# Three transformer layers on one core: attention results that come out turned, with the probabilities scaled ahead of the product

## The chip, the cores and the metric

The kernel runs on one core of a Trainium2 chip. The metric is the device time of one execution in microseconds (us). One execution computes a whole forward pass of three layers for one sequence of 256 rows and width 1024.

The core has five engines with a queue each: TensorE (PE in the rows; its weight loads are PEld), VectorE (DVE), ScalarE (ACT), GpSimd (POOL) and SyncE (SP), which issues the loads of the weights. They meet only through semaphores. TensorE writes to PSUM, eight banks of 128 partitions x 512 f32.

## The reference, cut to what matters

There are four attentions. All have 256 queries and 256 keys.

```
moba   8 heads of 64,  causal        \  first layer
cross  4 heads of 256, no mask       /
dsa    8 heads of 64,  causal and a learned choice of keys   second layer
mla   16 heads of 64 (scores over 96), causal                third layer

p = softmax(scores)               # over the keys
o = p @ v                         # per head
x = x + rms_norm(concat(o) @ w_out)
```

The first layer has a retention beside moba (4 heads of 128), whose result goes through a norm of each head and a gate, and the second one a short convolution with a gate beside dsa. Each shares the output projection with its attention: half of the rows of `w_out` belong to each. An MLP follows in each layer.

## The kernel before, in words

**Rows and tokens.** The 256 tokens are two tiles (`t` = 0, 1) of 128. An activation has its tokens on the partitions, `x[:, t, :]`. A projection needs it turned, with the features on the partitions: `hT[:, chunk, token]`, eight chunks of 128 features. TensorE turns blocks of 128 x 128 against an identity (`turn`, L1658), four of them to one PSUM bank; ScalarE and VectorE take them out.

**Large products.** A number is split in two fp32r numbers, hi and lo, and each product is made three times: hi x hi, lo x hi, hi x lo (`products`, L1589). Turned activations come as `hT_hi` (ScalarE, L603) and `hT_lo` (VectorE, L1077: PSUM less hi). Weights come by DMA in units of 128 x 2048 f32; ScalarE writes `w_hi` (L585), VectorE `w_lo` (L1056, L1059, L1062). `split_to(u)` in the lists of ScalarE and VectorE says where in their order this is done for unit u. Ring buffers hold four units.

**Attention** (`attention`, one function on each of PE, DVE and ACT). Each engine runs over the heads; these are the steps for a head `hd` of a causal attention, all in plain f32, of which TensorE makes two passes for each product (x2 in the counts of the rows):

1. PE `scores` (L1696): keys 0 to 127 for token tile 0, keys 0 to 255 for tile 1, so 384 columns in one PSUM bank (two banks in turn).
2. DVE (L1207): two instructions, of 128 and 256 columns, scale and mask the scores into SBUF (`S`), and take the row's extreme.
3. ACT (L748): two exponentials into `E`, with the sums of the rows in `a.sums`.
4. PE `turn_probs` (L1704), two heads behind the scores: three turns of 128 x 128 into a bank.
5. DVE `copy_turned` (L1219): 384 columns to `ET` in SBUF.
6. PE `values` (L1713), three heads behind: for each of the three blocks a product with 128 columns of `ET` as the stationary operand and the 64 columns of v as the moving one, into columns of the head in a bank with tokens on the partitions.

Cross has full blocks: four turns of a head, and four products with 256 moving columns. It takes the scores from PSUM, the extreme by L1211.

**Behind the last head.** The results in PSUM are unscaled. VectorE inverts the sums (L1236, L1253), and multiplies PSUM by them into `h` or `mix` in SBUF (L1237, L1255); TensorE turns these blocks (L1658), 8 for moba and dsa, 16 for cross and mla; ScalarE and VectorE write `hT_hi` and `hT_lo`; then the output projection runs (`project`, `out_project`). For cross and mla this is done in two halves of 512 features: the second one is turned behind the first unit of the projection. In moba the turns stand behind the first two score products of the retention (`meanwhile` in `retention`), in dsa within the projection, which begins with the convolution's features.

**Retention.** PE L1744 (scores) and L1752 (values), DVE L1369 (decay) between them. Then ACT squares (L869), DVE sums the squares of each head (L1375), POOL makes the inverse roots (L484, L485, 8 columns), DVE scales and gates (L1383), and PE turns the result within the output projection. The VectorE's list has a unit's `w_lo` (`split_to(n["used"] + 3)`, L1056) between L1375 and L1383.

**Convolution.** POOL makes three taps (`convolve`, L502 to L505). ACT copies the turned gate from PSUM (L947, into `gbT`), POOL multiplies (L507), ACT writes hi (L953), and POOL lo (L510).

**Latent rows of the third layer** (L1499 to L1540). DVE `copy_latents(t)` copies 384 query columns, and then waits for a norm by POOL (L522 to L525) before it writes the rest; `low_queries(1)` stands behind it in VectorE's list, and PE waits for that. POOL spreads a rotated key of 32 rows to 15 heads in one copy (L515).

What sets the order is written by hand: each engine's list, and the waits in it. `tb_ready` and `tb_free` hand the four turn banks (PSUM 4 to 7) round.

## Time and profile before

| | us |
|---|---|
| median of 3 runs | 1061.05 (1058.54 to 1062.13) |
| profiled execution | 1060.72 |
| its span, first to last instruction | 1058.9 |
| PE busy | 1032.3 (97%) |
| DVE busy | 647.0 (61%) |
| ACT busy | 565.5 (53%) |
| POOL busy | 85.4 (8%) |

The profiled execution took 1060.72 us; 1058.9 of these lie between its first and its last instruction. An engine's busy time is the sum of its instructions. For PE the ends of the instructions are modelled and overlap, so the distance between the starts of two groups says more than their durations. TensorE's granted clock was 0.996 of 2.4 GHz over the span.

### The profile page before, as it was taken

What the parts mean: (1) busy time and instruction counts of PE and PEld (TensorE: products, weight loads), DVE (VectorE), ACT (ScalarE), POOL (GpSimd) and SP (SyncE); (2) the same over time, 40 slices, a digit from 0 to 9 for tenths busy, and PEclk for the clock granted to TensorE, in tenths of its full rate; (3) what the DMA queues carried; (4) which work ended last, traced back from release to release, by engine and by line L of the source; (5) the groups of instructions that cost most, each with busy time, mean ns of one, the idle gap of its engine ahead of it and who ended that gap; (6) DMA issues with size and microseconds to landing.
All of it is one profiled execution on the core that took longest, in us unless ns stands there. A gap on an engine that the chain in (4) does not pass through costs nothing.

```text
span 1058.9 us, 13808 instructions
## 1 busy us (share of the span) xinstructions
PE 1032.3 (97%) x5074; PEld 867.6 (82%) x5074; DVE 647.0 (61%) x1007; ACT 565.5 (53%) x860; POOL 85.4 (8%) x109
## 2 busy tenths in 40 slices
PE   7999999999999999999999999999998999999997
PEld 6888878887888888788888888888897888888886
DVE  5575665446656455758846755455579767555553
ACT  7566455427545544756655744545466557454541
POOL 2010101001000000200061100000051000000000
PEclk9999999999999999999999999999999999999999
DMA  8746126414455454453433555544255035554521
GB/s 337 292 162 238 58 91 230 157 40 165 173 198 184 179 216 178 156 230 115 157 127 119 221 197 189 195 176 165 83 189 209 1 148 210 196 197 171 188 80 40
DMA packets 28461, 176.29 MB, mean 166 GB/s; under 512 B 3248, under 2 KB 3392, under 8 KB 9984
## 3 DMA queue, kind: packets, MB, share of 16 engines
q1 hardware_dynamic: 26784, 170.08, 43.6%
q0 software_dynamic: 1456, 5.48, 1.4%
q8 instruction: 29, 0.48, 0.2%
q10 hardware_dynamic: 176, 0.13, 0.0%
q14 instruction: 16, 0.13, 0.0%
HBM read 174.62 MB, written 1.05 MB: 166 GB/s over the span
## 4 chain that ended last, share of the span: by engine, by line
PE 90%; DVE 4%; ACT 2%; issue 2%; POOL 1%; DMA 1%; SPq 0%; DVEq 0%; ACTq 0%; POOLq 0%
PE PS L1589 77%; PE PS L1658 3%; PE PS L1696 3%; PE PS L1713 3%; PE PS L1803 2%; ACT w_hi L585 1%; PE PS L1704 1%; PE PS L1953 1%; DVE w_lo L1062 1%; DMA x<-in_x 1%; ACT work L665 0%; DVE w_lo L1059 0%; DVE w_lo L1056 0%; POOL rstd L485 0%; DVE arena L1095 0%
## 5 line engine op out<-in xcount | busy, mean ns | idle before, releaser
L1062 DVE SCALAR_TENSOR_TENSOR w_lo<-w_raw,gcol,w_hi 128x512 fp32r<-128x512 f32 (+4 forms) x318 | 261.2, 879 | 182.7 <-ACT w_hi L585 182.1
L585 ACT ACTIVATE w_hi<-w_raw,gcol 128x512 fp32r<-128x512 f32 (+4 forms) x326 | 244.5, 817 | 103.4 <-PE PS L1589 102.4
L1589 PE MATMUL PS<-w_hi,hT_hi 128*128 128x512 f32 (+2 forms) x888 | 243.4, 394 | 4.9 <-issue 2.4
L1589 PE MATMUL PS<-w_hi,hT_lo 128*128 128x512 f32 (+2 forms) x888 | 236.2, 386 | 0.0
L1589 PE MATMUL PS<-w_lo,hT_hi 128*128 128x512 f32 (+2 forms) x888 | 234.2, 384 | 0.2 <-DVE w_lo L1056 0.2
L1589 PEld LDWEIGHTS PS<-w_hi,hT_lo 128*128 128x128 f32 x888 | 165.6, 189 | 32.8
L1589 PEld LDWEIGHTS PS<-w_lo,hT_hi 128*128 128x128 f32 x888 | 164.9, 188 | 33.1 <-DVE w_lo L1056 0.6
L1589 PEld LDWEIGHTS PS<-w_hi,hT_hi 128*128 128x128 f32 x888 | 161.6, 190 | 35.8 <-DVE hT_lo L1077 1.9
L1056 DVE TENSOR_TENSOR w_lo<-w_raw,w_hi 128x2048 fp32r<-128x2048 f32 (+1 forms) x70 | 135.9, 1956 | 86.7 <-ACT w_hi L585 86.7
L585 ACT ACTIVATE w_hi<-w_raw 128x2048 fp32r<-128x2048 f32 (+1 forms) x70 | 114.6, 1644 | 109.4 <-PE PS L1589 109.4
L1589 PE MATMUL PS<-w_hi,gT_hi 128*128 128x512 f32 x408 | 113.9, 392 | 0.0
L1589 PE MATMUL PS<-w_lo,gT_hi 128*128 128x512 f32 x408 | 112.9, 390 | 0.0
L1589 PE MATMUL PS<-w_hi,gT_lo 128*128 128x512 f32 x408 | 112.7, 389 | 0.0
L1589 PEld LDWEIGHTS PS<-w_hi,gT_lo 128*128 128x128 f32 x408 | 76.6, 188 | 16.0
L1589 PEld LDWEIGHTS PS<-w_lo,gT_hi 128*128 128x128 f32 x408 | 76.5, 188 | 15.9
L1589 PEld LDWEIGHTS PS<-w_hi,gT_hi 128*128 128x128 f32 x408 | 76.2, 188 | 15.4
L484 POOL TENSOR_SCALAR msq<-ssq 128x1 f32<-128x1 f32 (+1 forms) x31 | 12.9, 418 | 823.2 <-ACT work L665 760.9
L603 ACT ACTIVATE hT_hi<-PS 128x512 fp32r<-128x512 f32 (+2 forms) x46 | 25.4, 582 | 42.7 <-PE PS L1658 42.7
L1077 DVE TENSOR_TENSOR hT_lo<-PS,hT_hi 128x512 fp32r<-128x512 f32 (+2 forms) x46 | 29.5, 668 | 26.8 <-ACT hT_hi L603 26.6
L748 ACT ACTIVATE work<-work,attention_bias 128x128 f32<-128x128 f32 x64 | 28.5, 447 | 26.0 <-DVE attention_bias L1207 26.0
L1141 DVE TENSOR_TENSOR work<-PS,gain 128x512 f32<-128x512 f32 x28 | 18.0, 684 | 39.7 <-ACT work L665 39.7
L665 ACT ACTIVATE work<-PS 128x1024 f32<-128x1024 f32 x14 | 14.4, 1028 | 49.7 <-PE PS L1589 49.7
(171 smaller groups left out, 811.5 us busy)
## 6 DMA issues: line engine op xcount, KB each, us to landing
w_raw<-in_w SPq DMA_DIRECT2D x64, 1024.0 KB, 4.8
w_raw<-in_w_gu SPq DMA_DIRECT2D x22, 1024.0 KB, 4.8
w_raw<-in_w_in SPq DMA_DIRECT2D x11, 1024.0 KB, 7.8
w_raw<-in_w_dn SPq DMA_DIRECT2D x22, 512.0 KB, 5.2
w_raw<-in_w_mem_k SPq DMA_DIRECT2D x4, 1024.0 KB, 4.8
w_raw<-in_w_out SPq DMA_DIRECT2D x4, 1024.0 KB, 4.8
w_raw<-in_w_cq SPq DMA_DIRECT2D x4, 1024.0 KB, 4.8
w_raw<-in_w_mem_v SPq DMA_DIRECT2D x4, 1024.0 KB, 4.8
```

The lines of the kernel that those rows point to most:

```text
L585: ins = act.activation(high, source, ACT.Copy, scale=1.0 if col is None else gcol[:, col + TURNED * k:col + TURNED * k + 1])
L603: act.activation(d, PS[:, 4 + n["tb"] % 4, 0:blocks * P].rearrange("p (b m) -> p b m", m=P), ACT.Copy).then_inc(tb_high, 1)
L748: ins = act.activation(a.E[hd % 3][:, c0:c1], src, ACT.Exp, bias=a.nb[:, hd, t:t + 1], scale=-1.0 if a.masked else a.scale, accum_out=a.su ...
L1056: ins = dve.tensor_tensor(lo, raw, hi, ALU.subtract)
L1062: ins = dve.scalar_tensor_tensor(out=lo, in0=raw, scalar=gcol[:, col + TURNED * k:col + TURNED * k + 1], in1=hi, op0=ALU.mult, op1=ALU.sub ...
L1077: dve.tensor_tensor(lo, PS[:, 4 + n["tb"] % 4, 0:blocks * P].rearrange("p (b m) -> p b m", m=P), hi.bitcast(F32), ALU.subtract).then_inc(t ...
L1141: steps.mark(dve.tensor_tensor(work[:, 2 * t + i, :], PS[:, 2 * t + i, :], gain[:, g, cols], ALU.mult))
L1589: mm = pe.matmul(bank(t, j)[:, 0:width], rows[:, kc0 + k, tok], w[:, s, at:at + width], start=begin and i == 0, stop=end and i == 2)
L1658: mm = pe.transpose(PS[0:rows, 4 + n["tb"] % 4, i * P:(i + 1) * P], src, ident[:])
L1696: mm = pe.matmul(PS[:, a.score_bank + hd % 2, c0:c1], q, k, start=i == 0, stop=i == len(pairs) - 1)
L1713: mm = pe.matmul(out_banks(a, t)[:, hd * a.dv:(hd + 1) * a.dv], a.ET[hd % 2][:, c0 + s * P:c0 + (s + 1) * P], a.v(hd, s), start=s == 0, st ...
L1803: mm = pe.transpose(m.turn_bank[t][:, b * P:(b + 1) * P], hidden[:, t, b * P:(b + 1) * P], ident[:])
```

## The change

The products of probabilities and values swap their operands. Two names need an explanation: `a.lag` is the number of heads by which `turn_probs` stands behind the scores (3 for causal attentions, 2 for cross), `a.ring` the number of buffers.

- VectorE inverts the sums of each head (`invert`), and GpSimd multiplies the head's probabilities in place by them (`normalise`, two instructions of a head), before TensorE turns them.
- The products have v as the stationary operand. For heads of 64, two heads share a group: one goes to partitions 0 to 63 of the result, the other to 64 to 127. The moving columns are 256 and 128 of `ET`. For cross the stationary operand is 128 columns of v and the moving one 256 columns of `ET`.
- The result lies in PSUM with features on the partitions. ScalarE writes `hT_hi` from it (`high_results`), VectorE `hT_lo` (`low_results`). The multiplications by the sums, the rows in `h` and `mix`, and their 48 turns are gone.
- `S` is gone: DVE writes masked scores to `E`, and ACT the exponentials in place. `E` and `ET` have four buffers each in causal attentions (three `S`, three `E` and two `ET` before), three each in cross.
- Retention: `split_to(n["used"] + 3)` stands before the sums of squares in VectorE's list. The turns of the memory's key rows are in two parts, around the turns of the retention's result.
- Convolution: DVE multiplies by the gate straight from PSUM, between two heads; ACT writes hi in two instructions and DVE lo in two, in place of POOL's five.
- Latent rows: the copy of the query columns and `low_queries(1)` stand before the wait for the norm. The rotated key is spread in five copies of three heads. `attention(mla, [0])` stands before `split_to(e + 9)` in VectorE's list.

```diff
@@ Attention @@
-                scored = 3 * width if causal_blocks else 0
-                self.S, self.E, self.ET = slots(0, 3), slots(scored, 3), slots(scored + 3 * width, 2)
+                self.ring = 4 if causal_blocks else 3
+                self.lag = 3 if causal_blocks else 2
+                self.group = P // dv if dv < P else 1
+                self.banks = heads * dv // 256
+        def result_bank(a, b):
+            return PS[:, a.out_bank + b, :].rearrange("p (c m) -> p c m", m=SEQ)
+        def result_rows(tile, b):
+            return tile[:, 2 * b:2 * b + 2, :]
@@ gpsimd @@
-                pool.wait_ge(gate_copied, TT)
-                pool.tensor_tensor(y_conv, y_conv, gbT, ALU.mult).then_inc(conv_ready, 1)
-                for c in range(4):
-                    pool.wait_ge(conv_high, c + 1)
-                    pool.tensor_tensor(hT_lo[:, 4 + c, :], y_conv[:, c, :], hT_hi[:, 4 + c, :].bitcast(F32), ALU.subtract).then_inc(conv_low, 1)
+            def normalise(a):
+                for hd in range(a.H):
+                    pool.wait_ge(a.inverted, hd + 1)
+                    for t in range(TT):
+                        place = a.E[hd % a.ring][:, slice(*a.cols[t])]
+                        ins = pool.tensor_scalar(place, place, a.sums[:, hd, t:t + 1], None, ALU.mult)
+                    ins.then_inc(a.normed, 1)
-                pool.tensor_copy(kT4[64:96, 1:16, :], kT4[64:96, 0:1, :].to_broadcast([32, 15, SEQ])).then_inc(rope_spread, 1)
+                for head in range(1, 16, 3):
+                    pool.tensor_copy(kT4[64:96, head:head + 3, :], kT4[64:96, 0:1, :].to_broadcast([32, 3, SEQ])).then_inc(rope_spread, 1)
@@ scalar @@
+            def high_results(a, banks=None):
+                for b in banks or range(a.banks):
+                    act.wait_ge(a.summed, (b + 1) * a.H // a.group // a.banks)
+                    act.activation(result_rows(hT_hi, b), result_bank(a, b), ACT.Copy).then_inc(a.high, 1)
...
-            attention(mla, range(2, mla.H), False)
-            high_halves(hT_hi)
+            attention(mla, range(2, 8), False)
+            for b in range(2):
+                attention(mla, range(8 + 4 * b, 12 + 4 * b), False)
+                high_results(mla, [b])
+            high_results(mla, [2, 3])
@@ vector @@
+                def invert(hd):
+                    dve.wait_ge(a.probs, hd + 1)
+                    dve.reciprocal(a.sums[:, hd, :], a.sums[:, hd, :]).then_inc(a.inverted, 1)
...
-                for hd in heads or range(a.H + 2):
+                for hd in heads or range(a.H + a.lag):
                     if hd < a.H:
                         masked_max(hd)
-                    elif rows is not None:
-                        normalise_half(a, rows, hd - a.H, 0)
-                    if hd >= 2:
-                        copy_turned(hd - 2)
+                    if 1 <= hd <= a.H:
+                        invert(hd - 1)
+                    if hd >= a.lag:
+                        copy_turned(hd - a.lag)
+            def low_results(a, banks=None):
+                for b in banks or range(a.banks):
+                    dve.wait_ge(a.high, b + 1)
+                    dve.tensor_tensor(result_rows(hT_lo, b), result_bank(a, b), result_rows(hT_hi, b).bitcast(F32),
+                                      ALU.subtract).then_inc(a.low, 1)
@@ retention @@
                 if hd == 1:
-                    low_banks(2, half_rows(0))
+                    low_results(moba)
+            split_to(n["used"] + 3)
             for t in range(TT):
                 dve.wait_ge(ret_sq, t + 1)
                 dve.tensor_reduce(...)
-            split_to(n["used"] + 3)
@@ dsa @@
-            attention(dsa, range(dsa.H + 2), False)
-            normalise(dsa, h)
+            attention(dsa, range(5), False)
+            for t in range(TT):
+                dve.wait_ge(gate_turned, t + 1)
+                dve.wait_ge(convolved, 1)
+                dve.tensor_tensor(y_conv[:, :, token_cols(t)], PS[:, t, :].rearrange("p (b m) -> p b m", m=P), y_conv[:, :, token_cols(t)],
+                                  ALU.mult).then_inc(conv_ready, 1)
+            attention(dsa, range(5, dsa.H + dsa.lag), False)
+            for t in range(TT):
+                dve.wait_ge(conv_high, t + 1)
+                dve.tensor_tensor(hT_lo[:, 4:8, token_cols(t)], ..., ALU.subtract).then_inc(conv_low, 1)
+            low_results(dsa)
@@ latent rows @@
+            copy_queries(0)
             copy_latents(0)
...
+            copy_queries(1)
+            low_queries(1)
             copy_latents(1)
-            low_queries(1)
@@ tensor @@
                 def turn_probs(hd):
-                    pe.wait_ge(a.probs, hd + 1)
+                    pe.wait_ge(a.normed, hd + 1)
...
+                def values(g):
+                    pe.wait_ge(a.copied, a.group * (g + 1))
+                    if a.masked:
+                        for s in range(2):
+                            for i in range(2):
+                                hd = 2 * g + i
+                                mm = pe.matmul(result_bank(a, g // 2)[64 * i:64 * i + 64, g % 2, P * s:SEQ], a.v(hd, s),
+                                               a.ET[hd % a.ring][:, 2 * P * s:SEQ + P * s], start=s == 0, stop=s == 1)
+                    else:
+                        probs = a.ET[g % a.ring].rearrange("p (t s m) -> p t s m", t=TT, s=2)
+                        for i in range(2):
+                            for s in range(2):
+                                mm = pe.matmul(result_bank(a, g)[:, i, :], a.v(g, s)[:, P * i:P * i + P], probs[:, :, s, :],
+                                               start=s == 0, stop=s == 1)
                     mm.then_inc(a.summed, 1)
-                for hd in heads or range(a.H + 3):
+                for hd in heads or range(a.H + a.lag + 1):
                     if hd < a.H:
                         scores(hd)
-                    if 2 <= hd < a.H + 2:
-                        turn_probs(hd - 2)
-                    if hd >= 3:
-                        values(hd - 3)
-                    if rows is not None and hd == a.H + 1:
-                        turn_half(rows, 0)
+                    if a.lag <= hd < a.H + a.lag:
+                        turn_probs(hd - a.lag)
+                    done = hd - a.lag
+                    if done >= 1 and done % a.group == 0:
+                        values(done // a.group - 1)
...
+            def results(a, banks):
+                return lambda: pe.wait_ge(a.low, banks)
+            def out_project(a):
+                project(4, 2, wide, hooks={(0, 0): results(a, 2), (0, 2): results(a, 3), (0, 3): results(a, 4), (1, 2): tile0})
```

## Rows read from the trace of the kernel before

**Rows 1.** Page, busy time; and the chain that ended last, by engine.
```profile
PE 1032.3 (97%) x5074; PEld 867.6 (82%) x5074; DVE 647.0 (61%) x1007; ACT 565.5 (53%) x860; POOL 85.4 (8%) x109
PE 90%; DVE 4%; ACT 2%; issue 2%; POOL 1%; DMA 1%; SPq 0%; DVEq 0%; ACTq 0%; POOLq 0%
```
**Rows 2.** Busy us (x count) of PE, PEld, DVE, ACT, POOL in four stretches.
```profile
107.09:118.42 11.33, 11.30 (x89) 10.50 (x90) 6.86 (x28) 7.56 (x25) 0.00 (x0) 1.00 0.17 71
125.17:136.37 11.20, 8.68 (x52) 7.08 (x50) 8.12 (x15) 3.48 (x6) 3.82 (x2) 0.99 0.26 95
546.80:558.90 12.10, 12.06 (x97) 11.26 (x97) 6.68 (x27) 8.57 (x27) 5.21 (x5) 1.00 0.00 1
819.03:845.12 26.09, 25.55 (x202) 23.72 (x202) 17.87 (x73) 14.67 (x58) 0.00 (x0) 1.00 0.01 5
```
**Rows 3.** Timeline of one head in mla: start, duration, engine, line, idle before.
```profile
828.03 0.49 PE L1704 MATMUL PS<-ident,work 128*128 128x128 f32 x3
828.23 0.29 DVE L1207 CUSTOM_DVE_ANT_0 work<-PS,causal 128x128 f32<-128x128 f32 x1 [0.54 <-PE PS L1696]
828.25 0.75 PEld L1713 LDWEIGHTS PS<-arena,work 128*128 128x128 f32 x6
828.36 0.78 PE L1713 MATMUL PS<-arena,work 128*128 128x64 f32 x6
828.79 0.55 DVE L1219 COPY work<-PS 128x384 f32<-128x384 f32 x1
828.98 0.87 PE L1696 MATMUL PS<-arena 128*128 128x128 f32 x4
829.43 0.19 ACT L748 ACTIVATION_READ_ACCUMULATOR work<-work,attention_bias 128x1 f32 x1
829.69 0.49 PE L1704 MATMUL PS<-ident,work 128*128 128x128 f32 x3
```
**Rows 4.** Timeline of the end of cross, PE and DVE.
```profile
211.39 1.89 PE L1713 MATMUL PS<-arena,work 128*128 128x256 f32 x8
213.12 0.60 PE L1704 MATMUL PS<-ident,work 128*128 128x128 f32 x4
213.32 0.18 DVE L1236 RECIPROCAL attention_sum<-attention_sum 128x4 f32<-128x4 f32 x1 [2.85 <-PE PS L1713]
214.88 1.99 PE L1713 MATMUL PS<-arena,work 128*128 128x256 f32 x8 [1.16 <-DVE work L1219]
216.71 1.04 PE L1658 MATMUL PS<-ident,h 128*128 128x128 f32 x8
217.58 1.89 PE L1713 MATMUL PS<-arena,work 128*128 128x256 f32 x8
```
**Rows 5.** The chain that ended last, about retention and mla's projection: start, us, what.
```profile
127.45 2.18 POOL msq L484
129.70 1.66 POOL rstd L485
849.65 1.93 ACT w_hi L585
```
**Rows 6.** Timeline of mla's projection, TensorE's weight loads, idle before them.
```profile
846.55 0.30 PEld L1589 LDWEIGHTS PS<-w_hi,hT_hi 128*128 128x128 f32 x2 [0.24 <-DVE h L1237]
853.95 0.77 PEld L1589 LDWEIGHTS PS<-w_lo,hT_hi 128*128 128x128 f32 x4 [0.58 <-DVE w_lo L1056]
```
**Rows 7.** Groups of GpSimd by line.
```profile
L505 POOL TENSOR_TENSOR arena<-arena 128x1020 f32<-128x1020 f32 x1 | 4.3, 4301 | 0.1
L505 POOL TENSOR_TENSOR arena<-arena 128x1016 f32<-128x1016 f32 x1 | 2.0, 1992 | 0.1
L551 POOL MEMSET arena<- 128x2048 f32 x1 | 1.8, 1820 | 44.6 <-ACT arena L910 44.6
```
**Rows 8.** Timeline of the latent rows, before mla.
```profile
787.30 0.59 PE L1589 MATMUL PS<-w_hi,hT_hi 128*128 128x384 f32 x2 [0.97 <-DVE hT_lo L1077]
795.10 5.86 DVE L1059 SCALAR_TENSOR_TENSOR w_lo<-w_raw,gcol,w_hi 128x512 fp32r<-128x512 f32 x4
```

More of the change, by code:

```diff
@@ L542, in _ @@
             norms(TT)
+            normalise(moba)
             inverse_root(128, RETENTION, 8, ret_ss, TT, ret_rstd)
-            for _ in range(3):
+            for i in range(3):
                 norms(2 * TT)
                 load_gain()
+                if i == 0:
+                    normalise(cross)
             for i in range(2):
@@ L1360, in _ @@
             split_to(n["used"] + 2)
-            attention(moba, range(1, moba.H + 2), False)
+            attention(moba, range(1, moba.H + moba.lag), False)
             dve.wait_ge(decay_loaded, 16)
-            normalise(moba, mix)
             for hd in range(4):
@@ L1398, in _ @@
             split_to(n["used"] + 2)
-            attention(cross, range(1, cross.H + 2), False, h)
+            attention(cross, range(1, cross.H + cross.lag), False)
+            low_results(cross)
             split_to(n["used"] + 3)
-            out_rows(cross)
             boundary(1, 4)
@@ L1553, in _ @@
             copy_values(0)
+            attention(mla, [0])
             split_to(e + 9)
-            attention(mla, [0])
             copy_keys(1)
@@ L1558, in _ @@
             copy_values(1)
-            attention(mla, range(2, mla.H + 2), False, h)
-            out_rows(mla)
+            attention(mla, range(2, 13), False)
+            low_results(mla, [0])
+            attention(mla, range(13, 17), False)
+            low_results(mla, [1])
+            attention(mla, range(17, mla.H + mla.lag), False)
+            low_results(mla, [2, 3])
             boundary(5, 4)
@@ L1683, in turn_stream, with attention @@
                     turn([x[:, t, P * (4 * half + b):P * (4 * half + b + 1)] for b in range(4)])
-            def attention(a, heads=None, rows=None):
+            def attention(a, heads=None):
                 def scores(hd):
@@ L1931, in _ @@
             copied()
-            attention(cross, range(3, cross.H + 3), h)
-            out_project(h)
+            attention(cross, range(3, cross.H + cross.lag + 1))
+            out_project(cross)
             mlp(ffn, between={(2, 0): half_of(0, 0)})
@@ L2073, in _ @@
             pe.wait_ge(values_copied, 4)
-            attention(mla, range(3, mla.H + 3), h)
-            out_project(h)
+            attention(mla, range(3, mla.H + mla.lag + 1))
+            out_project(mla)
             mlp(mlps[1])
```

142 lines of the change are left out of this document (54 added, 88 removed).

## Prediction

> **What bounds the kernel now.** I read the page's busy times and chain first: TensorE is busy for 97% of the span and is 90% of the chain that ended last [rows 1]. So the change is worth what it takes from TensorE's queue, or from the waits in it, and VectorE, ScalarE and GpSimd have room to give. The table by stretch says the same of the four attentions: in moba, dsa and mla TensorE idles for 0.03, 0.04 and 0.54 us. The one large hole is the output projection behind the retention, 2.52 of 11.20 us [rows 2]. Then the timeline of one head in mla's steady part gives the prices [rows 3]: turns of the probabilities 828.03 to 828.36 (0.33 us), values 828.36 to 828.98 (0.62), scores 828.98 to 829.69 (0.71). That is 1.66 a head, 3.31 a pair, with no gap.
>
> Three prices of a pass follow. Eight turns of 128 columns take 216.71 to 217.58, 0.109 each. In cross eight passes of 256 columns take 211.39 to 213.12, 0.216 each [rows 4]. So a pass streams at 0.85 ns a column. But a value pass of only 64 columns costs 0.62 / 6 = 0.103, not 0.054 [rows 3]: its 128 stationary columns must be loaded, and that sets its pace. That is what the change turns round.
>
> **Values of a head of 64.** After it, a pair of heads needs for each head two passes of 256 columns and two of 128, with 64 stationary columns: 2 x (2 x 0.216 + 2 x 0.108) = 1.30 us if all stand one behind another. Before it was 1.24. So by itself the swap gains nothing; the point is the two halves of the columns. In program order the passes are A A B B (256 columns), A A B B (128). If a pass of one half may run beside one of the other, but each starts in order, this takes three slots of 0.216 and two of 0.108: 0.86 us. No row of before shows two passes side by side. The bounds are 0.65 (full overlap) and 1.30 (none); a price above 1.30 is a rival below. I take 0.86, since nothing in the order of the passes needs more.
>
> The Trainium skill (TensorEngine Tiling (Array Packing), Key Properties) says that tiles run in parallel, but also that a change of the tiling mode drains TensorE, which this change does twice a pair; the second rival stands beside that.
>
> **VectorE and the order in a pair.** VectorE needs 0.56 us for the extremes of a head and 0.55 for the copy (828.23 to 828.79, and the copy) [rows 3], and now a reciprocal: 0.18 with its latency for 4 columns [rows 4], I take 0.10 to 0.18 of its queue. That is 1.25 to 1.3 a head, 2.6 a pair, below TensorE's 2 x (0.71 + 0.33) + 0.86 = 2.94. But the values of a pair wait for the copy of its second head. From the end of the scores before: 0.2 to VectorE's start, 0.56 + 0.1 + 0.55 and 0.1 back, 1.5, against 0.33 + 0.71 + 0.33 = 1.37 of TensorE's work. So some 0.15 of stall: 3.09 a pair, a gain of 0.22.
>
> **GpSimd.** A head of 384 columns in two instructions. Memset writes 2048 columns in 1.82 us, 0.89 ns a column; a product with two inputs takes 1.99 for 1016 and 4.30 for 1020 where VectorE worked beside it on two SBUF inputs [rows 7]. So 0.5 to 1.1 us, 2.4 at the worst. I take 0.8, with one input nearer to the memset. VectorE has no instruction with two SBUF inputs in the steady part (scores and copies come from PSUM). Three heads of lag give 3 x 1.55 = 4.6 us from scores to turn; the chain needs about 1.4 to the last exponential's end (scores' end 828.2 to 829.62 in the pattern of [rows 3]), some 0.6 until VectorE's turn comes for the reciprocal, and 0.8 to 1.1. It is hidden, except behind the last scores.
>
> **The end of a causal attention.** It is longer now. From the end of the last scores: the chain of the last head gives scaled probabilities after 3.0 to 3.3 us; in the meantime TensorE has two pairs of values and three turns (2.7) but waits for copies that stand behind the last reciprocal. The last turn ends at about 3.95, its copy 0.75 later, the last values at 5.65. Before it was 3.95 in moba (three turns, four values, gaps of 0.17 twice).
>
> - moba, from 107.09: five scores, four turns, one pair and a stall of 0.3 (6.03), then 5.65: 11.7 against 11.33. **+0.4.**
> - dsa: as moba, plus 0.87 for the gate's turns. VectorE now has the two products with the gate (0.68 each by the nearest form, PSUM to SBUF of 512 columns) between two heads. That makes it late for the copy before the second pair: 0.8 of stall on TensorE. Behind the last copy stand the convolution's two lo parts, 1.36, and the projection waits for them: 0.5 more than the values need. 6.03 + 0.87 + 0.8 + 5.65 + 0.5 = 13.85 against 12.1, **+1.7**; and 8 turns leave the projection, -0.87. GpSimd's taps end before the first head needs its scaling, so that queue costs nothing here. Sum **+0.8**.
> - mla, from 819.03: first head 1.04, six pairs of 3.09, less the last values and turn (1.19), which the end counts again, and 5.65: the projection begins at 843.1 in place of 845.12, -2.0. The second 8 turns go, -0.87; so does a wait for them (0.24) and one of 0.58 for a unit's `w_lo` [rows 6], which came late because ScalarE split this unit only behind those turns, at 849.65 [rows 5]. Sum **-3.7**.
>
> **Cross** has no halves: four products of 256 columns before and after, 1.73. Its 16 turns leave, 16 x 0.109 = 1.75. VectorE multiplied by the sums while TensorE waited for a copy behind it, 1.16 idle [rows 4], and this goes: 2.9. What comes: GpSimd twice 256 columns, 0.5 to 1.2 us, within the 4.3 us that TensorE works between the last scores and the last turn. hi and lo of the first two banks are written during the last values, those of the last within the projection's first units (2.7 us each). Late next: nothing by more than 0.1. Sum **-2.9**, between -2.3 and -3.0.
>
> **Retention.** Here the chain is sums of squares, GpSimd's two instructions, VectorE's scaling, turn, hi, lo. GpSimd's first took 2.18 us beside a `w_lo` of VectorE and its second 1.66 [rows 5]; with `w_lo` ahead of the sums the first should fall to some 0.3. But the sums now wait for the end of `w_lo`, 0.3 to 0.5 late. So the scaling starts 1.6 earlier by the retention's own clock. TensorE has 8.07 us of work in these 11.20 (two units of 2.73 and 24 turns), so 3.1 of waiting by its starts; with half of the key turns moved between the last result's turn and its lo, 1.15 of it should be left, -2.0. Eight turns (0.87) leave the retention itself, but VectorE's decay and lo stand in for most of them: -0.3. Sum **-2.3** (between -1.0 and -3.0).
>
> **Latent rows.** TensorE waited 0.97 for `hT_lo` [rows 8]; with the query rows ahead of the norm it comes 0.7 earlier, **-0.7**, if what follows (VectorE's rotations) moves up too; if not, 0. The spread in five copies is the same work; VectorE's four lo instructions took 5.86 beside it [rows 8]. Smaller pieces can give or cost 1; I take 0. The swap of `attention(mla, [0])` and the split only reorders a full queue: 0.
>
> **Sum.** +0.4 - 2.3 + 0.8 - 2.9 - 3.7 - 0.7 = -8.4. The profiled execution took 1060.72 us (1058.9 of span and 1.8 around it, which I leave as it is), 0.3 below the median of the runs: 1060.7 - 8.4 = 1052.3, and on the median's scale 1052.6. I give **1052.5**.
>
> **The rivals.**
>
> *The halves don't run side by side.* A pair costs 1.30. For it: no row shows two passes together. Against it: nothing but the layout, which puts them in different columns. The stall before the values vanishes, so a steady pair of mla costs 3.38: six times +0.29, 1.7; each end has two pairs in it, +0.88 in moba and in mla; and dsa, where TensorE waits for VectorE anyway, pays about 1.0. In all 4.5 more: **1057**, still faster by what cross, retention and the last turns bring.
>
> *A change of the array's shape costs (slower).* Place: before and behind each of 16 pairs of values. If the array empties at each, with the 64-column loads not hidden either: two times 0.17 (a pass of 64 columns lasts about 0.27 in the rows where its pace is 0.103) and eight loads of 0.053 on top of 1.30, so 2.06 a pair, 1.05 over my sum with its stall: +16.8, **1069**. It decides from 1.56 us a pair on. Against it: in the rows loads run beside passes of the same rows of the array (PEld from 828.25 beside the turns' 828.03 to 828.52) [rows 3].
>
> That page's neighbour in the Trainium skill (TensorE: Matmul & The Clock Gate, Part 3, The mechanism) says that a weight load overlaps a running product only where the row group differs; by that rule these loads would not be hidden. The trace disagrees for full tiles, and shows nothing for halves; by the two rules together the time would be 1069, by the rows 1052.5.
>
> *GpSimd becomes the bound.* If it needs 2.4 us a head as beside VectorE's two-input work [rows 7], 0.85 over TensorE's 1.55, some 23 heads pay: +20, 1072. From 1.55 a head it decides. Against it: VectorE reads PSUM there.
>
> **How the numbers follow.** Halves side by side 0.60 (with gaps up to 1.0 a pair and the retention uncertain: 1048 to 1055). One behind another 0.24. Shape change 0.10. GpSimd 0.06. The range, 1047 to 1061, leaves out most of the last two and little below. 0.3% is 3.2 us, about what a measurement of this kernel can tell from no change. Faster: nearly all of the first (0.59) and most of the second (0.19), 0.78. Within: 0.12. Slower: what the last two hold beyond +3.2, 0.10.
>
> **What would show it.** Right: value groups of a pair within 0.9 us and pairs of mla at 3.1; the page with 48 turns less; waits behind the retention near 1.15 in place of 3.1; cross shorter by 2.9. GpSimd at 0.8 a head, never releasing a turn except for the last head. Wrong: a pair of values of 1.3 or more; TensorE's turns released by GpSimd in mid-attention; VectorE above 1.5 a head. The prediction fails if the ends of the attentions cost 2 us more each than I gave.

## The result, and the profile after

The changed kernel takes 1053.1 us in the median of 4 runs (1052.3 to 1055.7), the kernel before 1061.4 in the runs beside them: a ratio of 0.9936, interval 0.9911 to 0.996. Forecast were 1052.5, so the time is right to 0.6 us. The sum behind it came out partly by luck: some terms were too good, and a gain that was not in the sum made up for part of them.

The page of the kernel after, its busy times and the chain that ended last, answers to [rows 1]; then, from the groups by line, the new work:

```profile
PE 1023.1 (97%) x4962; PEld 849.3 (81%) x4962; DVE 641.8 (61%) x1029; ACT 564.1 (54%) x856; POOL 135.0 (13%) x180
PE 87%; DVE 5%; POOL 3%; ACT 2%; issue 2%; DMA 1%; SPq 0%; DVEq 0%; ACTq 0%
L521 POOL TENSOR_SCALAR work<-work,attention_sum 128x256 f32<-128x256 f32 x40 | 36.8, 921 | 42.8 <-DVE attention_sum L1235 42.8
L521 POOL TENSOR_SCALAR work<-work,attention_sum 128x128 f32<-128x128 f32 x32 | 19.3, 602 | 59.5 <-DVE attention_sum L1235 58.9 <-POOL arena L512 0.2
```

TensorE has 112 instructions less: the 48 turns, and 4 of 12 value passes in each of 16 pairs. GpSimd (POOL) has 56 us more work in line 521, the scaling, and is now in the chain with 3%. A head of 384 columns costs it 0.60 + 0.92 = 1.52 us by these means (4.46 for three in the timeline below, 1.49 each), a head of cross 1.84. The prediction had 0.8 and 0.5 to 1.2.

The stretches of the kernel after that answer to those of [rows 2], busy us (x count) of PE, PEld, DVE, ACT, POOL, then TensorE's granted clock:

```profile
107.78:120.68 12.90, 10.47 (x76) 7.19 (x77) 7.54 (x34) 8.03 (x26) 10.37 (x14) 1.00 0.15 62
126.70:135.81 9.11, 8.46 (x51) 7.10 (x50) 6.79 (x15) 3.31 (x6) 1.87 (x2) 1.00 0.34 117
544.14:558.45 14.31, 11.42 (x85) 8.15 (x85) 9.99 (x39) 8.54 (x25) 8.94 (x12) 1.00 0.00 0
816.21:841.32 25.11, 22.99 (x164) 15.89 (x164) 18.34 (x85) 15.04 (x59) 22.60 (x31) 1.00 0.03 13
```

Before, TensorE idled 0.03 us in moba and 0.04 in dsa; now it idles 2.4 and 2.9, and 2.1 in mla (first number less PE's busy time). In the second row it is the other way: 11.20 has become 9.11, and 2.52 of idle 0.65.

Cut at the first scores of each attention and at the output projections, the timelines of TensorE give the whole account. Each number is the distance between two starts, in us. Before and after were each profiled twice; the last column is the version without the scaling, below.

| stretch | before | before again | after | after again | no scaling |
|---|---|---|---|---|---|
| to moba | 98.50 | 99.71 | 99.19 | 98.60 | 97.56 |
| moba and retention | 26.67 | 26.66 | 27.51 | 27.53 | 25.68 |
| projection to cross | 70.81 | 70.91 | 67.23 | 67.21 | 67.25 |
| cross | 23.14 | 23.14 | 22.16 | 22.17 | 20.84 |
| projection to dsa | 315.78 | 314.19 | 316.49 | 313.29 | 314.84 |
| dsa | 24.03 | 24.04 | 25.87 | 25.87 | 24.17 |
| projection to mla | 251.31 | 251.30 | 248.98 | 249.02 | 248.98 |
| mla | 34.88 | 34.87 | 33.89 | 33.92 | 31.78 |
| projection to the end | 213.78 | 213.88 | 212.58 | 212.59 | 212.24 |

Every attention repeats within 0.03 us. The stretch before dsa does not: it takes 3.2 us more in one profile of after than in the other. Busy times and granted clock for 455 to 460 us, first of the kernel after, then of its second profile:

```profile
455.00:460.00 5.00, 5.00 (x23) 4.71 (x23) 2.60 (x12) 2.41 (x8) 0.00 (x0) 0.53 0.58 213
```

```profile
455.00:460.00 5.00, 5.00 (x35) 4.46 (x34) 4.02 (x13) 3.51 (x9) 0.00 (x0) 1.00 0.58 213
```

TensorE is busy all the time in both, but in the first it ran close to its lower level of 1.2 GHz (0.53 of 2.4) and made 23 passes in place of 35. The runs of the kernel after spread from 1052 to 1056 accordingly. The kernel before does the same: its granted clock from 460 to 465 us was 0.66 in one profile and 1.00 in the other, and its stretch took 315.78 and 314.19. So I compare by stretches.

### The profile page after: what moved, and what is told of

Same layout as the page of the kernel before. It is cut to its first block, busy times and chain, and to the rows that moved or that the text cites. A ratio compares the mean times of both kernels' runs of the same rounds, so it can differ in the third digit from the quotient of the medians.

```text
span 1053.9 us, 13628 instructions
## 1 busy us (share of the span) xinstructions
PE 1023.1 (97%) x4962; PEld 849.3 (81%) x4962; DVE 641.8 (61%) x1029; ACT 564.1 (54%) x856; POOL 135.0 (13%) x180
## 3 DMA queue, kind: packets, MB, share of 16 engines
HBM read 174.62 MB, written 1.05 MB: 167 GB/s over the span
## 4 chain that ended last, share of the span: by engine, by line
PE 87%; DVE 5%; POOL 3%; ACT 2%; issue 2%; DMA 1%; SPq 0%; DVEq 0%; ACTq 0%
PE PS L1607 78%; PE PS L1676 3%; POOL work L521 2%; PE PS L1826 2%; PE PS L1714 1%; ACT w_hi L603 1%; PE PS L1977 1%; DVE w_lo L1080 1%; DVE w_lo L1074 1%; PE PS L1722 1%; DMA x<-in_x 1%; DVE w_lo L1077 1%; PE PS L1732 1%; PE PS L1738 0%; ACT work L683 0%
## 5 line engine op out<-in xcount | busy, mean ns | idle before, releaser
L521 POOL TENSOR_SCALAR work<-work,attention_sum 128x128 f32<-128x128 f32 (+1 forms) x72 | 54.9, 780 | 102.3 <-DVE attention_sum L1235 101.8
L794 ACT ACTIVATE arena<-PS,rstd 128x512 f32<-128x512 f32 x32 | 22.1, 690 | 32.6 <-PE PS L1607 32.1
```

Of the source, the lines that this page charges most:

```text
L521: ins = pool.tensor_scalar(place, place, a.sums[:, hd, t:t + 1], None, ALU.mult)
L794: act.activation(part_tile[:, t, :], m.up_bank[t], ACT.Relu, scale=scale).then_inc(m.part, 1)
```

## The experiments

All are variants of the kernel after unless it says otherwise. Ratios are to the kernel before, which ran beside each: 1060.7 us in the median beside after once more, the version without the scaling, the halves in turn and ScalarE's share; 1060.9 beside one half, 128 columns, three engines and the retention's edits on before; 1061.2 beside the others.

**After once more.**

> The changed kernel again, beside the others. Theory (GpSimd sets the pace of the causal attentions: two instructions of a head take 1.49 us, so a pair of heads 2.98, and TensorE waits for them behind the last scores): 1053 us, pairs of mla 3.0 to 3.1 apart, GpSimd releases TensorE about 8 times, 5 us in all. Rival (the copy before a pair's values sets it, as I had forecast): the same time, but TensorE's gaps in mid-attention end with VectorE. Its granted clock: where 80 columns a pass run (near 455 us) it fell to 0.61 to 0.69 in one profile; if that is chance of the run, it differs here.

1054.1 us (1051.9 to 1056.2), ratio 0.9942 (0.9922 to 0.9963). It is the fourth column above, and shows the spread: the clock near 455 us differs, as its last sentence asked. GpSimd releases TensorE 8 times, as in the first profile, and no wait of TensorE in mid-attention ends with VectorE, so the theory held.

**Without the scaling.** GpSimd's list skips `normalise`, and TensorE waits for the reciprocal.

```diff
-                    pe.wait_ge(a.normed, hd + 1)
+                    pe.wait_ge(a.inverted, hd + 1)
```

> GpSimd's scaling is left out (the output lacks the division by the sums), TensorE's turns wait for VectorE's reciprocal alone. GpSimd sets the pace: a pair of mla falls from 3.0 to 2.9 or less (TensorE's own 2 x 1.04 + 0.80 = 2.88), each of the three causal ends gets 1.2 to 1.9 shorter and moba's start 0.4, so 4 to 6 us less than the changed kernel, 1048. Rival (GpSimd hidden): pairs stay at 3.0, only the ends gain, 0.5 each: 1051.5.

1045.2 us (1044.9 to 1045.5), ratio 0.9853 (0.9836 to 0.9869): 8.9 below after in the medians, 7.0 in the four rows of the attentions. That is more than the 4 to 6 expected, since 1.3 of it is in cross, which the expectation left out. TensorE's waits by engine, for after and then without the scaling (us, times, longest):

```profile
PE PS L1722 <- POOL work L521: 5.0, 8, 0.9
PE PS L1732 <- DVE work L1241: 2.0, 3, 0.7
```

```profile
PE PS L1727 <- DVE work L1236: 3.2, 7, 0.7
```

Where GpSimd's work sits in the chain is plain at the end of moba, in the timeline of after (start, duration, idle before):

```profile
114.17 4.46 POOL L521 TENSOR_SCALAR work<-work,attention_sum 128x128 f32<-128x128 f32 x6 [0.15 <-DVE attention_sum L1235]
115.72 0.55 PE L1722 MATMUL PS<-ident,work 128*128 128x128 f32 x3 [0.27 <-POOL work L521]
117.20 0.55 PE L1722 MATMUL PS<-ident,work 128*128 128x128 f32 x3 [0.93 <-POOL work L521]
118.68 0.55 PE L1722 MATMUL PS<-ident,work 128*128 128x128 f32 x3
119.88 0.87 PE L1732 MATMUL PS<-work,arena 128*64 128x256 f32 x8 [0.65 <-DVE work L1241]
```

GpSimd works without a gap through three heads, and the turns of the last three heads start 1.48 us apart, GpSimd's price. From the start of the last scores to the end of moba it takes 7.20 us, without the scaling 5.91. The last wait, 0.65 for VectorE's copy, is there with and without the scaling.

GpSimd also shows in mla's steady part, which TensorE's waits above leave out. Without the scaling every steady pair takes 2.99 us, from values to values; after takes 3.10 and 2.99 by turns. The weight load of one turn in each pair then waits for GpSimd (timeline of PEld, after):

```profile
828.59 0.31 PEld L1722 LDWEIGHTS PS<-ident,work 128*128 128x128 f32 x3 [0.21 <-POOL work L521]
831.69 0.31 PEld L1722 LDWEIGHTS PS<-ident,work 128*128 128x128 f32 x3 [0.31 <-POOL work L521]
```

**The halves one behind the other in program order.** All four passes of one head, then those of the other:

```diff
-                        for s in range(2):
-                            for i in range(2):
+                        for i in range(2):
+                            for s in range(2):
```

> The same passes, all four of one head before all four of the other. If the halves run side by side only where a pass of the other half follows in program order, a pair of values takes about 1.2 in place of 0.80, a pair of mla 3.3 in place of 3.0, and the time rises by 3 to 5 us, to 1057. Rival (the 0.80 comes from something else, such as cheaper passes with 64 stationary columns): values stay at 0.80 and the time at 1053.

1055.9 us (1052.7 to 1056.3), ratio 0.9944 (0.9927 to 0.9961): as after, and its attentions take what they take in after, within 0.05. The theory missed and the rival held. The timeline shows a group of values 0.81 us ahead of the next scores, as in after (0.80):

```profile
829.66 0.88 PE L1732 MATMUL PS<-work,arena 128*64 128x256 f32 x8
830.47 0.92 PE L1714 MATMUL PS<-arena 128*128 128x128 f32 x4
```

From this I took it that the halves don't run side by side at all, and that 64 stationary columns are simply cheaper. The next two test that.

**Both heads in one half; and 128 stationary columns.** First, both heads of a pair write partitions 0 to 63. Then, `a.v2` is the 128 columns of v of both heads, so that no pass has 64 stationary columns. Both keep the order of the last experiment, one head behind the other, which by itself cost nothing.

```diff
-                                mm = pe.matmul(result_bank(a, g // 2)[64 * i:64 * i + 64, g % 2, P * s:SEQ], a.v(hd, s),
+                                mm = pe.matmul(result_bank(a, g // 2)[0:64, g % 2, P * s:SEQ], a.v(hd, s),
```

```diff
+                                mm = pe.matmul(result_bank(a, g // 2)[:, g % 2, P * s:SEQ], a.v2(g, s),
```

> The kernel after, but both heads of a pair write the same half of the array's columns (partitions 0 to 63 of the result, so the second head overwrites the first and the upper 64 rows of the results are not computed); stationary operands stay 64 columns wide, one head's passes behind the other's. Theory of the prediction (passes in the two halves run side by side): without halves side by side a pair costs 1.30 us in place of 0.80, and the time is some 4.5 us longer than after. Theory that stands since the run with the halves in turn (a pass with 64 stationary columns streams at half the price a column whatever half it is in): a pair stays at 0.80 us, and the time within 1.5 us of after.

> The kernel after, but the stationary operand of each value product is 128 columns wide (the values of both heads of the pair), with the same moving columns and the same number of passes; the second head's result overwrites the first's, so the results are wrong. Theory (64 stationary columns halve the price of a moving column): a pair costs 4 x 0.216 + 4 x 0.108 = 1.30 us in place of 0.80, and as the copy of the second head is no longer waited for, a steady pair of mla is 3.3 to 3.4 us against 3.0; time 4 to 7 us above after. The 0.1 to 0.2 us of idle without a releaser in front of the scores behind a group of values goes if it belongs to the change of the array's shape. Rival (price of f32 passes is set by something else, such as the moving columns alone): pair and time as after.

One half: 1061.1 us (1060.1 to 1062.3), ratio 1.0004 (0.9995 to 1.0013). 128 columns: 1057.4 (1056.9 to 1057.6), 0.9969 (0.9957 to 0.9981). The timelines of a pair in mla, of after, of one half, and of 128 columns:

```profile
828.62 0.52 PE L1722 MATMUL PS<-ident,work 128*128 128x128 f32 x3
829.07 0.87 PE L1732 MATMUL PS<-work,arena 128*64 128x256 f32 x8
829.87 0.92 PE L1714 MATMUL PS<-arena 128*128 128x128 f32 x4
830.63 0.49 PE L1722 MATMUL PS<-ident,work 128*128 128x128 f32 x3
832.17 0.87 PE L1732 MATMUL PS<-work,arena 128*64 128x256 f32 x8
```

```profile
828.50 1.51 PE L1732 MATMUL PS<-work,arena 128*64 128x256 f32 x8
829.95 0.92 PE L1714 MATMUL PS<-arena 128*128 128x128 f32 x4
830.71 0.49 PE L1722 MATMUL PS<-ident,work 128*128 128x128 f32 x3
832.14 0.43 PE L1732 MATMUL PS<-work,arena 128*64 128x256 f32 x1
```

```profile
828.63 1.57 PE L1735 MATMUL PS<-work,arena 128*128 128x256 f32 x8
830.04 0.82 PE L1717 MATMUL PS<-arena 128*128 128x128 f32 x4
830.70 0.49 PE L1725 MATMUL PS<-ident,work 128*128 128x128 f32 x3
832.13 1.57 PE L1735 MATMUL PS<-work,arena 128*128 128x256 f32 x8
```

The same eight passes with the same 64-column loads cost 0.80 us with a head in each half and 1.45 with both in one: 0.65 more, which is just the 768 columns of one head at 0.85 ns. So the halves do run side by side, fully, and 64 stationary columns by themselves are no cheaper. The trace shows it directly too. These are the first 0.25 us of such a group, instructions of its line alone (PE busy (x count), PEld, clock), for after, the halves in turn, one half, and 128 columns:

```profile
829.06:829.30 0.24, 0.23 (x2) 0.20 (x4) 1.00 0.00 0
829.65:829.90 0.25, 0.24 (x2) 0.20 (x4) 1.00 0.00 0
828.49:828.74 0.25, 0.24 (x1) 0.19 (x2) 1.00 0.13 33
828.62:828.87 0.25, 0.24 (x1) 0.24 (x2) 1.00 0.00 0
```

Two passes run where there are two halves, one where there is one. My intermediate theory fell, and that of the prediction stands, but for the order: since all of one head before all of the other costs the same (0.81, where starts in program order would need some 1.2), a pass isn't held back until its predecessor in the other half has started. The price is 0.65 + 0.15, not 0.86 from an order of starts. Of the 0.15, 0.11 stands in the third fence too (1.41 against 1.30), so little of it belongs to the halves.

By stretches, one half costs 1.75 us over after in moba, 0.70 in dsa and 4.06 in mla, 6.5 in all.

The second and third fences together give the price of changing the array's shape. A pair costs 3.64 us with 64 columns in one half and 3.50 with 128: 0.14 a pair, of which 0.10 is in the scores behind the values (0.76 against 0.66 to the next turn). Over moba, dsa and mla the two kernels differ by 2.5 us for 16 pairs, 0.15 each. They also differ in the width of the loads, 64 columns against 128, which I take to be hidden in both.

**ScalarE scales the first tile of the causal heads**, behind the exponentials of the next head; GpSimd the second tile, and all of cross.

```diff
+            def scale_first(a, hd):
+                act.wait_ge(a.inverted, hd + 1)
+                place = a.E[hd % a.ring][:, 0:P]
+                act.activation(place, place, ACT.Copy, scale=a.sums[:, hd, 0:1]).then_inc(a.first, 1)
```

> ScalarE scales the first 128 columns of each causal head, GpSimd only the other 256 (0.92 us). GpSimd sets the pace: now 1.84 a pair, TensorE is the bound at 2.9, and behind the last scores two or three waits of 0.57 each go: 3 to 4 us less, 1049.5. Rival (GpSimd hidden): no gain, or 0.5 us more because ScalarE has another instruction in its queue.

1049.7 us (1049.5 to 1050.5), ratio 0.9898 (0.9881 to 0.9914). moba and retention took 26.08, dsa 24.36, mla 32.20, so 4.7 us below after in all, with cross unchanged at 22.15. The theory held, and all steady pairs of mla take 2.99 us, as without the scaling.

**Three engines.** As the last, with ScalarE on the first tile of cross too, and VectorE on the second tile of cross and of the last head of each causal attention.

```diff
+                    if not a.masked or hd == a.H - 1:
+                        dve.wait_ge(a.inverted, hd + 1)
+                        place = a.E[hd % a.ring][:, slice(*a.cols[1])]
+                        dve.tensor_scalar(place, place, a.sums[:, hd, 1:2], None, ALU.mult).then_inc(a.second, 1)
```

> The kernel after with the scaling spread over three engines: ScalarE scales the first tile of every head, VectorE the second tile in cross and of the last head of each causal attention, GpSimd the second tile of the other causal heads. Theory (GpSimd's 1.49 us a causal head and 1.83 a cross head cost at the ends of the attentions and in cross): the waits of the turns for GpSimd go in cross (1.0 us) and shrink by some 0.5 us at the end of each causal attention against the version in which ScalarE scales only the first tile of causal heads (1049.7 us): 1046.5 to 1048. The floor is the version without any scaling, 1045.2. Rival (what that version gained is its floor, and ScalarE or VectorE become late instead): 1049 to 1051.

1050.1 us (1049.5 to 1051.1), ratio 0.99 (0.9884 to 0.9916): the rival's range. Cross gave 0.47 (21.68), but the causal attentions lost 0.26, 0.26 and 0.24. At their ends the turn now waits for ScalarE (0.34 in moba) and the copy behind VectorE's extra work comes late (0.16).

**The best of these**, with the last pair of values but one behind the last turn, so that it covers the last copy:

```diff
+                    if a.masked and done == a.H - 1:
+                        values(a.H // 2 - 2)
```

> A version meant to be faster than both: ScalarE scales the first tile of every head, GpSimd the second of the causal heads, VectorE the second of cross's; and in the causal attentions the last pair of values but one stands behind the last turn, so that it hides the last copy. Theory: against the version with ScalarE's share alone (1049.7 us) cross gives 0.5 us, as in the version with three engines, and each of the three ends 0.2 to 0.4 us of the 0.65 us for which TensorE waits there for the last copy: 1048.2 to 1048.9. Rival (the last turn waits for GpSimd anyway, and the values that filled this wait now stand behind it): the ends give nothing, 1049.2 to 1049.7.

1047.6 us (1047.3 to 1048.8), ratio 0.9878 (0.9864 to 0.9892): faster than both kernels, and 2.1 below the version with ScalarE's share alone. The stretches give moba 25.71, cross 21.67, dsa 24.01, mla 32.16, which is 1.2 of these 2.1; the rest lies outside the attentions. The end of mla in its timeline:

```profile
830.89 0.69 DVE L1268 TENSOR_TENSOR hT_lo<-PS,hT_hi 128x512 fp32r<-128x512 f32 x1 [0.47 <-ACT hT_hi L782]
831.08 0.52 PE L1735 MATMUL PS<-ident,work 128*128 128x128 f32 x3 [0.38 <-POOL work L522]
831.50 1.01 DVE L1253 COPY work<-PS 128x384 f32<-128x384 f32 x2
831.52 0.87 PE L1745 MATMUL PS<-work,arena 128*64 128x256 f32 x8
832.57 0.87 PE L1745 MATMUL PS<-work,arena 128*64 128x256 f32 x8 [0.17 <-DVE work L1253]
```

The wait of 0.65 is 0.17 in mla, and none in moba and dsa. There the reordering gave 0.37 and 0.35, in mla 0.04. The wait for GpSimd is about the same in all three (0.38, 0.42, 0.38). What only mla has is a `hT_lo` of VectorE just ahead of the last two copies, so that they end late.

**The retention's edits alone, on the kernel before; and the kernel after without them.** The `w_lo` on VectorE and the key turns on TensorE:

```diff
+            split_to(n["used"] + 3)
             for t in range(TT):
                 dve.wait_ge(ret_sq, t + 1)
...
-            split_to(n["used"] + 3)
...
-                turn_rows(k_tok, False)
+                turn_rows(k_tok, False, [0])
                 turn_half(mix, 512)
-                turned(2)
+                turn_rows(k_tok, False, [1])
```

> The kernel before with the edits of the retention alone: the w_lo of the third unit ahead of the sums of squares on VectorE, and the key turns in two parts. Theory (the reorder brings the gain behind the retention, and a shorter hole keeps TensorE's clock): GpSimd's first instruction falls from 2.18 to 0.2-0.4 us, TensorE's waits in the projection from 2.5-3.1 to 0.6-1.2 us, so the projection's first part is 2.0 us shorter, and the granted clock behind the hole stays at 1.00, worth another 1.5 us: time 3.0 to 3.8 us below the kernel before. Rival (the clock's fall was chance and is no part of the effect): 1.7 to 2.3 us below, with the granted clock behind the hole 1.00 in some profiles of before as well. Rival (the gain came from the 8 turns that left the retention): 0 to 0.7 us below.

> The kernel after with the two edits of the retention undone (w_lo behind the sums of squares on VectorE, the key turns in one part). Theory (a hole of 3 us behind the retention costs its own length and then TensorE's clock for some microseconds): GpSimd's first instruction takes 1.8 to 2.2 us again, the projection's first part 11.0 to 11.3 us in place of 9.1, and the granted clock falls below 1.00 behind the hole; the time is 3.3 to 4.0 us above after, so 1057 to 1058. Rival (the clock's fall in the profile of before was chance): 1.8 to 2.3 us above, with a granted clock of 1.00 behind the hole.

> The kernel before once more, for a second profile of it. Theory: from the projection behind the retention to the first scores of cross it takes 70.8 us as in the first profile, with the granted clock below 1.00 just behind the hole in both; the stretch from the output projection of cross to the first scores of dsa, in which the clock falls about 455 us, takes another of the values seen (0, 1.6 or 3.2 us over the shortest). Rival: the clock's fall behind the hole is missing in this profile, and the first stretch is 69.3 us.

Before with the edits: 1057.3 us (1056.7 to 1058.4), ratio 0.9968 (0.9957 to 0.998), so some 3.4 us, as expected. Its projection ran 9.11 us to the end of the hole as in after, and GpSimd's first instruction took 0.20 in place of 2.18 [rows 5]; VectorE then releases TensorE after 0.67 us of idle:

```profile
128.07 0.20 POOL L484 TENSOR_SCALAR msq<-ssq 128x8 f32<-128x8 f32 x1 [62.05 <-DVE ssq L1377]
134.45 1.17 PE L1591 MATMUL PS<-w_hi,hT_hi 128*128 128x512 f32 x4 [0.67 <-DVE hT_lo L1078]
```

After without the edits: 1057.7 us (1056.2 to 1060.0), ratio 0.9971 (0.9958 to 0.9983), 3.1 above the version with the old latent rows that ran beside it (1054.6). Before once more: 1060.5 us. The stretch from this projection to cross is 67.25 us for the first, 69.30 for the second and 70.91 for the third, where after has 67.23. The granted clock (third column from the end) behind the hole tells why, in the kernel before, before again, and after without the edits:

```profile
136.00:138.00 2.00, 1.63 (x4) 1.37 (x5) 0.27 (x1) 0.00 (x0) 0.00 (x0) 0.55 0.00 0
138.00:140.00 2.00, 2.00 (x6) 1.53 (x6) 0.00 (x0) 0.00 (x0) 0.00 (x0) 0.60 0.00 0
```

```profile
138.00:140.00 2.00, 2.00 (x8) 1.56 (x7) 0.00 (x0) 0.00 (x0) 0.00 (x0) 0.64 0.00 0
140.00:142.00 2.00, 2.00 (x7) 1.52 (x6) 0.00 (x0) 0.00 (x0) 0.00 (x0) 0.51 0.00 0
```

```profile
138.00:140.00 2.00, 2.00 (x10) 1.65 (x10) 0.00 (x0) 0.00 (x0) 0.00 (x0) 1.00 0.00 0
```

In all three TensorE idled for 1.06 or 1.07 and then 1.46 us, within 4 us, just before. The clock fell in two of them and not in the third. Of 39 further runs of the kernel before two took 1058 us, the others 1060.0 to 1062.3, so it may be spared seldom there; but these runs left no profile, and the clock near 455 us moves the time by as much. The shorter hole (0.65) was followed by a full clock in each of 11 profiles (67.19 to 67.25 us). So the hole itself costs 2.1 us, and mostly a further 1.5 to 1.6 in clock. What decides when it is spared, I can't say.

**The latent rows as before**, with the spread still in five copies:

```diff
             copy_queries(1)
-            low_queries(1)
             copy_latents(1)
+            low_queries(1)
```

> The kernel after, but on VectorE low_queries(1) stands behind copy_latents(1) again, so behind the wait for the norm, as in the kernel before; the spread of the rotated key stays in five copies. From the projection of dsa to mla the profile of before takes 251.31 us and every profile with the change 248.95 to 249.02: 2.3 us less, of which the 8 turns are 0.87. Theory (the reorder brings all the rest): that stretch grows by 1.2 to 1.5 us and the time by as much. Rival (the reorder brings only the 0.7 us that the prediction gave it, and the five copies the rest): it grows by 0.6 to 0.8 us.

1054.6 us (1051.9 to 1056.5), ratio 0.9934 (0.9915 to 0.9952): not to be told from after. The stretch from dsa's projection to mla grew from 248.98 to 249.24 us: 0.26, less than either expectation, so both missed. TensorE waits 0.96 for `hT_lo` again, as in [rows 8], where in after it waits 0.67 for VectorE's next instruction. The rest of the gain shows in VectorE's four lo instructions, in after:

```profile
793.46 4.43 DVE L1077 SCALAR_TENSOR_TENSOR w_lo<-w_raw,gcol,w_hi 128x512 fp32r<-128x512 f32 x4
793.69 5.71 POOL L528 COPY arena<-arena 32x768 f32<-32x768 f32 x5 [5.50 <-DVE hT_lo L1095]
```

They took 5.86 us [rows 8] beside one copy of 3.76 us, and take 4.43 beside five: 1.43 less. One by one, in before the second of the four took 3.88 us beside that copy and the others 0.74 each; in after three take 1.31 each, in turn with the copies. So the wait of 1.10 us for `w_lo` that TensorE had at 801.01 in before is gone. That the five copies are the cause is read from this overlap; they were not undone by themselves.

## Why the prediction was right, and where it wasn't

Its sum was -8.4, and the medians moved by 8.3. But the table of stretches gives only -7.3, with the clock near 455 us left out and the difference in the start too:

| term | predicted | measured |
|---|---|---|
| moba | +0.4 | +1.6 |
| retention and its projection | -2.3 | -2.8, and -1.5 of clock |
| cross, with 8 turns behind it | -2.9 | -1.9 |
| dsa, with 8 turns behind it | +0.8 | +1.0 |
| latent rows | -0.7 | -1.5 |
| mla and what follows | -3.7 | -2.2 |

The 8 turns behind cross and those behind dsa are put in with the prediction's own 0.87 each. In moba, cross and mla the sum was too good by 3.7 us. The retention and the latent rows gave 1.3 more than forecast, and the clock 1.5 that was not forecast at all. That the total agrees within 1.1 is partly luck, and the last 1.0 up to the medians lies in the stretches that are left out.

**Values of a pair: right.** 0.86 by the order of starts, 0.80 measured, halves side by side; the order of starts itself was wrong. The first rival, that they don't run so, is refuted; it was worth 6.5 us by stretches, more than the 4.5 it was given. In one half the kernel stands at 1061.1, no better than before: without the halves the other gains are just eaten up by what the scaling costs.

**Pairs of mla: right by luck.** Forecast were 3.09 us, from 2.94 of TensorE's own work and 0.15 of waiting for a copy. Measured are 3.10 and 2.99 by turns. Without the scaling a pair takes 2.99 (two turns and two scores 2.08, values 0.80, the shape 0.10), so no stall by the copy is left to see. The 0.11 in every second pair is GpSimd's.

**Shape change: right in kind, small in size.** The rival had 1.05 us a pair over my sum. It is 0.14 to 0.15 us a pair. The Trainium skill (TensorEngine Tiling (Array Packing), Key Properties) has both, tiles in parallel and a drain when the mode changes. The trace agrees: 0.65 us a pair saved by the halves, 0.14 lost with the shape. The Trainium skill (TensorE: Matmul & The Clock Gate, Part 3, The mechanism) also has the rule that a load overlaps a product only where the row group differs. Here the trace disagrees: the 64-column passes in one half keep 0.85 ns a column, with no load added.

**GpSimd: the mis-sized term.** 0.8 us a head was taken, 1.5 measured, and 1.84 in cross, above the range given. The guess came from the memset, 0.89 ns a column [rows 7]; the two points 0.60 and 0.92 us make 2.5 ns a column and 0.28 fixed. At 1.49 it is level with TensorE's own 1.50 a head (2.99 a pair), so it costs little in the steady pairs of mla (3.31 us before), and the cost appears where TensorE has nothing else to do: at the ends and in cross. From the start of the last scores to the end of the values mla's end took 7.26 us (834.06 to 841.32), where the prediction's 0.71 + 5.65 is 6.36; moba's took 7.20. Without the scaling it is 5.91. That puts moba at +1.6, takes 1.0 from mla, and 1.1 from cross: 22.16 in place of 21.1, and the kernel without scaling has 20.84. Its sentence "never releasing a turn except for the last head" is wrong: 8 waits in the page of waits, 5.0 us, of which 0.44 in moba (at 111.11) and 0.28 in mla (at 819.52) lie early in the attention. By the prediction's own list, turns released by GpSimd in mid-attention were a sign that it is wrong.

**Retention: right by its steps**, -2.1 behind and -0.7 in it (-2.0 and -0.3). The clock was not in the sum, though the trace of before showed it: 0.55 and 0.60 were granted from 136 to 140. It gave 1.5, less than half of what moba, cross and mla missed.

**Latent rows.** The step "with the query rows ahead of the norm it comes 0.7 earlier" was worth 0.26. "The spread in five copies is the same work" was the larger part: the same work, but VectorE isn't held for all of it.

**dsa and mla's last turns.** dsa was forecast with 13.85 to its projection, and took 14.31, for 12.1 before. The reason was another: the forecast put 0.8 on a copy that comes late behind the gate's products, but after has no such wait. Without the scaling dsa takes 24.17 us, 0.1 over before, so 1.7 of its 1.8 is the scaling: two turns wait 0.71 and 0.93 for GpSimd. Behind mla -1.2 is left of the 1.7 that its turns and two waits should give.

## What to carry to other kernels

Put two heads of 64 in the two halves of TensorE's columns: here eight f32 passes took 0.80 us in two halves and 1.45 in one, whatever their order, and the change of shape took 0.14. Work handed to an idle engine is nearly free in the steady part as long as its price a step stays below the bounding engine's (at 1.49 against 1.50 us it cost 0.11 in every second pair); at each end and each short stage its latency is paid (1.3 us at moba's end), so share it there among engines that are free. When a small wait is taken away, look at the granted clock behind it too: it can be worth most of the wait again.

## What the hardware showed that I had not expected

- A product by one value a partition, f32 in SBUF, takes GpSimd 0.60 us for 128 columns and 0.92 for 256, where VectorE takes 0.35 for the 256 (cross, three engines).
- VectorE's four instructions took 5.86 us beside one long copy of GpSimd, and 4.43 beside five shorter ones of the same volume. GpSimd itself pays for it, 5.71 in place of 3.76.
- TensorE's granted clock fell near 455 us in some executions and not in others of the same kernel, to a mean of 0.53 over 5 us at the lowest, with TensorE busy throughout; two profiles' spans differ by 3.7 us, of which 3.2 lie there.
